# Eight conditioning products moved from the sample attention into the prompt attention of a hybrid decoder step

## The reference

```
def adaln(c, w_ada, b_ada):                       # c: 1 prompt row, 8 sample rows of 1024
    m = jax.nn.silu(c) @ w_ada + b_ada            # w_ada: 1024 x 6144
    return jnp.split(m[:, None, :], 6, axis=-1)   # shift, scale and gate of two norms
...
h = modulated rms_norm(x)                         # uses two of the six parts
y = merge_groups(short_conv(h), nsa_attention(h)) @ w_out
x = x + gate * y                                  # the other four parts from here on
x = x + gate * hier_moe(modulated rms_norm(x))
```

## Time and profile before

| What | us |
|---|---|
| median of 3 runs (2212.95 to 2220.4) | 2215.51 |
| the profiled execution's own time | 2215.07 |
| its span | 2213.3 |
| PE busy (share of the span) | 1931.5 (87%) |
| DVE busy | 1278.9 (58%) |
| ACT busy | 1070.0 (48%) |
| POOL busy | 225.7 (10%) |

### The profile page before, as it was taken

One profiled execution on the slowest core, in us unless ns is written; L12 is line 12 of the kernel. 1 busy time (PEld: TensorE's weight loads), 2 busy tenths in 40 slices (PEclk: granted clock), 3 DMA queues, 4 the chain that ended last, 5 costly groups with the idle time before them and its releaser, 6 DMA issues. The chain is left out here.

```text
span 2213.3 us, 27531 instructions
## 1 busy us (share of the span) xinstructions
PE 1931.5 (87%) x9878; PEld 1497.0 (68%) x9878; DVE 1278.9 (58%) x1961; ACT 1070.0 (48%) x1671; POOL 225.7 (10%) x203
## 2 busy tenths in 40 slices
PE   6899995999979888887976899589999999997756
PEld 2799785999977677772222355468888888885642
DVE  1534424544445667672102566599888888885626
ACT  5312113444436677771110211278788787874532
POOL 0100001000002334330110000001000000000011
PEclk9999997999976799998988999699999999998877
DMA  8321127534037210015881722289999999987636
GB/s 288 78 96 44 48 79 264 217 150 160 8 80 217 63 25 5 6 45 136 244 201 43 285 100 95 105 329 413 425 421 413 415 414 414 412 343 284 248 129 264
DMA packets 155490, 443.05 MB, mean 200 GB/s; under 512 B 37384, under 2 KB 82380, under 8 KB 123712
## 3 DMA queue, kind: packets, MB, share of 16 engines
q1 hardware_dynamic: 136272, 340.82, 41.6%
q0 software_dynamic: 13792, 81.90, 10.8%
q10 hardware_dynamic: 5328, 19.02, 2.1%
HBM read 387.21 MB, written 58.70 MB: 201 GB/s over the span
## 5 line engine op out<-in xcount | busy, mean ns | idle before, releaser
L2782 DVE TENSOR_TENSOR moe_lo<-wts_raw,moe_hi 128x2048 fp32r<-128x2048 f32 x216 | 484.8, 2288 | 115.8 <-ACT moe_hi L2679 115.7
L2679 ACT ACTIVATE moe_hi<-wts_raw 128x2048 fp32r<-128x2048 f32 x216 | 402.7, 1915 | 93.8 <-DMA wts_raw<-in_w_gate 42.7
L949 DVE TENSOR_TENSOR cmp_xl<-cmp_bank,cmp_xh 128x512 fp32r<-128x512 f32 (+1 forms) x136 | 82.6, 668 | 121.0 <-ACT cmp_xh L903 121.0
L873 PE MATMUL cmp_hp<-cmp_xh,cmp_wh 128*128 128x256 f32 (+2 forms) x512 | 150.6, 294 | 0.0
L1375 POOL TENSOR_SCALAR att_prow<-att_prow,att_scale 128x640 f32<-128x640 f32 (+15 forms) x96 | 113.4, 1194 | 342.5 <-DVE att_scale L1499 342.5
L1472 DVE TENSOR_TENSOR att_pl<-att_pT,att_ph 128x512 fp32r<-128x512 f32 (+5 forms) x148 | 101.2, 688 | 79.7 <-ACT att_ph L1403 79.4
L873 PE MATMUL cmp_hp<-cmp_xh,cmp_wl 128*128 128x256 f32 (+2 forms) x512 | 146.6, 286 | 0.0
L873 PE MATMUL cmp_hp<-cmp_xl,cmp_wh 128*128 128x256 f32 (+2 forms) x512 | 146.4, 286 | 0.0
L2550 PE MATMUL moe_G<-moe_hi,moe_xh 128*128 128x512 f32 x288 | 118.1, 410 | 24.8 <-issue 21.7
L1984 POOL DMA_INDIRECT rou_xg<-s_h,rou_idx x36 | 51.2, 1422 | 826.2 <-PE moe_XT L2569 506.7
L2590 PE MATMUL moe_Y<-moe_hi,moe_hh 128*128 128x512 f32 x288 | 115.2, 400 | 19.0 <-issue 11.1
(11 more groups left out here) (455 smaller groups left out, 4391.1 us busy)
## 6 DMA issues: line engine op xcount, KB each, us to landing
wts_raw<-in_w_gate SPq DMA_DIRECT2D x72, 1024.0 KB, 7.0
wts_raw<-in_w_up SPq DMA_DIRECT2D x72, 1024.0 KB, 7.6
wts_raw<-in_w_down SPq DMA_DIRECT2D x72, 1024.0 KB
s_yb<-moe_y ACTq DMA_DIRECT2D x36, 512.0 KB, 7.7
fro_wraw<-in_w_ada SPq DMA_DIRECT2D x4, 2048.0 KB
s_yb<-att_zero SPq DMA_DIRECT2D x1, 8192.0 KB, 32.8
one_buf<-in_w_ada SPq DMA_DIRECT2D x4, 2048.0 KB
smp_wa<-in_w_ada SPq DMA_DIRECT2D x4, 2048.0 KB
```

The costliest lines, as they stand in the source:

```text
L873: last = pe.matmul(hp[u % 2][:, 0:n], lhs[:, w, :], rhs[:, u % 3, at], start=(r == 0 and t == 0 and m == 0), stop=(r == 1 and t == 7 and m ...
L2679: act.activation(hi[p][half][:, :], raw[p][half][:, :], ACT.Copy).then_inc(hi_ready[p], 1)
L2782: dve.tensor_tensor(lo[p][half][:, :], raw[p][half][:, :], hi[p][half][:, :], ALU.subtract).then_inc(lo_ready[p], 1)
```

## The change

The eight pieces leave the sample attention. In the prompt attention they become ring items, two for each pair 6 to 13 (tiles 3 to 6): `("cond", m, 0)` and `("cond", m, 1)`, each with half of a piece's 512 columns. Now 128x128 blocks of `w_ada` are the weights and the nine rows stream, so a half piece is two column blocks by eight row blocks. ACT copies the 128x18 result, DVE adds the bias. The bias arrives as 32 rows of 128 and is turned once at the start (`("bias",)`). After pair 14 the collected columns are turned back (`("mods",)`) and written to `s_mod` in eight transfers. The pieces are loaded into the buffers of the later gathers (`kvs`): the first two at `i == 1` ahead of `sample.load`, the others when the piece two before is through. The sample's compressed keys and values (`ck`, `cv`) and the constant `tri` are loaded in the prompt attention's last tile, into a buffer whose queries and masks are no longer needed; before, they were loaded at the start of the sample attention, or with `sample.load`.

```diff
+    NM, NC9 = ADA - ADA1, 4 * 9
+    P0 = 6
...
     for half in range(2):
         put(("q", 0, half))
+    put(("bias",))
...
             while backs:
-                order.append(("back", backs.pop(0)))
+                pair = backs.pop(0)
+                if 0 <= pair - P0 < NM:
+                    put(("cond", pair - P0, 1))
+                order.append(("back", pair))
+                if pair == P0 + NM:
+                    put(("mods",))
+            if k == 0 and groups[units[y][0]][1] == SEL and 0 <= units[y][0] // 3 - P0 < NM:
+                put(("cond", units[y][0] // 3 - P0, 0))
             for n in mine[len(mine) * k // QG:len(mine) * (k + 1) // QG]:
                 put_tile(n)
...
+            sp.dma_start(brow[:, :], a["b_ada"][:, ADA1 * 512:ADA * 512].rearrange("o (r c) -> (o r) c", c=P)).then_inc(brow_in, 16)
+            sp.dma_start(cT[:, :, :].rearrange("p k n -> p (k n)"), a["s_cT"]).then_inc(cT_in, 16)
+
+            def load_piece(m):
+                if m >= 2:
+                    sp.wait_ge(ring_full, ring_at[("cond", m - 2, 1)] + 1)
+                n = slice((ADA1 + m) * 512, (ADA1 + m + 1) * 512)
+                sp.dma_start(wa[m % 2], a["w_ada"][0, :, n].rearrange("(k p) n -> p k n", p=P)).then_inc(wa_in[m % 2], 16)
...
+                if P0 < 2 * i < P0 + NM:
+                    load_piece(2 * i - P0)
                 if i == 1:
+                    load_piece(0)
+                    load_piece(1)
                     sample.load(nc, a, sp)
...
-            sample.load_modulation(a, sp, tile.ada)
+                if P0 < 2 * i < P0 + NM:
+                    load_piece(2 * i - P0 + 1)
+            sp.wait_ge(ring_full, ring_at[("cond", NM - 1, 1)] + 1)
+            sample.load_compressed(a, sp, tile.buf)
+            sp.wait_ge(ring_free, ring_at[("mods",)] + 1)
+            mod_cols = a["s_mod"][:, ADA1 * 512:ADA * 512].rearrange("r (j x c) -> r x j c", x=8, c=P)
+            for x in range(8):
+                sp.dma_start(mod_cols[:, x, :, :], mrow[x * 9:(x + 1) * 9, :, :]).then_inc(mod_out, 16)
...
+                elif ring[r][0] == "bias":
+                    pe.wait_ge(brow_in, 16)
+                    last = pe.transpose(dst[:, 0, 0:4 * NM], brow[:, :], ident[0:4 * NM, 0:4 * NM])
+                elif ring[r][0] == "cond":
+                    _, m, half = ring[r]
+                    pe.wait_ge(cT_in, 16)
+                    pe.wait_ge(wa_in[m % 2], 16 * (m // 2 + 1))
+                    for t in range(2):
+                        cols = slice((2 * half + t) * P, (2 * half + t + 1) * P)
+                        for k in range(KT):
+                            last = pe.matmul(dst[:, 0, 9 * t:9 * t + 9], wa[m % 2][:, k, cols], cT[:, k, :],
+                                             start=(k == 0), stop=(k == KT - 1))
...
+                elif ring[r][0] == "cond":
+                    _, m, half = ring[r]
+                    at = m * NC9 + 18 * half
+                    act.wait_ge(ring_full, r + 1)
+                    act.activation(mT[:, at:at + 18], src[:, 0, 0:18], ACT.Copy).then_inc(ring_high, 1)
...
-            for m in range(MOD1):
-                condition(m)
...
-                if u in mod_after:
-                    condition(MOD1 + mod_after.index(u))
```

More of the change, by code:

```diff
@@ L1043, in __init__ @@
         self.slot8 = s.sb("slot8", [P, 16])
[L1044 to L1047, removed]
+        self.ck_in = s.sem("ck_in")
+        self.cv_in = s.sem("cv_in")
         self.const_in = s.sem("const_in")
@@ L1202, in stage_prompt_attention @@
         acc = [s.sb(f"acc{i}", [P, NH, HD]) for i in range(2)]
+        wa = [sample.kvs[:, 2 * i:2 * i + 2, :].rearrange("p i c -> p (i c)").rearrange("p (k n) -> p k n", n=512)
+              for i in range(2)]
+        cT = s.sb("cT", [P, KT, 9])
+        brow = s.sb("brow", [4 * NM, P])
+        bT = s.sb("bT", [P, 4 * NM])
+        mT = s.sb("mT", [P, NM * NC9])
+        mrow = s.sb("mrow", [2 * NC9, NM // 2, P])
         S = s.ps("S", [P, NB_S * 512])
@@ L1210, in stage_prompt_attention @@
         q_in = [s.sem(f"q_in{i}") for i in range(2)]
+        cT_in = s.sem("cT_in")
+        brow_in = s.sem("brow_in")
+        wa_in = [s.sem(f"wa_in{i}") for i in range(2)]
+        mod_out = s.sem("mod_out")
         masks_ready = s.sem("masks_ready")
@@ L1292, in fill @@
                         last = pe.transpose(dst[:, t, :], q[i % 2][:, half * 4 + t, :], ident[:, :])
+                elif ring[r][0] == "bias":
[10 more added lines that the diff above has]
+                                             start=(k == 0), stop=(k == KT - 1))
+                elif ring[r][0] == "mods":
+                    pe.wait_ge(ring_free, ring_at[("cond", NM - 1, 1)] + 1)
+                    for j in range(NM // 2):
+                        last = pe.transpose(dst[0:2 * NC9, j, :], mT[:, 2 * NC9 * j:2 * NC9 * (j + 1)], ident[:, :])
                 else:
@@ L1468, in low_part @@
                                              op0=ALU.mult, op1=ALU.subtract).then_inc(ring_free, 1)
+                elif ring[r][0] == "bias":
+                    dve.tensor_copy(bT[:, 2 * NM:4 * NM], src[:, 0, 2 * NM:4 * NM]).then_inc(ring_free, 1)
+                elif ring[r][0] == "cond":
+                    _, m, half = ring[r]
+                    at = m * NC9 + 18 * half
+                    c = 4 * m + 2 * half
+                    dve.wait_ge(ring_free, ring_at[("bias",)] + 1)
+                    piece = mT[:, at:at + 18].rearrange("p (b r) -> p b r", r=9)
+                    dve.tensor_tensor(piece, piece, bT[:, c:c + 2].rearrange("p (b o) -> p b o", o=1).to_broadcast([P, 2, 9]), ALU.add
+                                      ).then_inc(ring_free, 1)
+                elif ring[r][0] == "mods":
+                    dve.tensor_copy(mrow[:, 2:4, :], src[0:2 * NC9, 2:4, :]).then_inc(ring_free, 1)
                 else:
@@ L1568, in stage_sample_attention @@
         tri = given.tri
-        cT = given.cT
-        ones9 = s.sb("ones9", [1, 9])
-        wa = [tile.ada, s.sb("wa1", [P, KT, 512])]
-        ba = [given.ba, s.sb("ba1", [1, 512])]
-        mrow = [s.sb(f"mrow{i}", [9, 512]) for i in range(2)]
         rank = s.sb("rank", [P, NCK])
```

78 lines of the change are left out of this document (20 added, 58 removed).

## The result

The changed kernel takes 2272.72 us (median of 4 runs, 2270.06 to 2276.09), the kernel before beside it 2214.23 us: a ratio of 1.0266, 95% interval 1.0232 to 1.0300. It is slower by 58 us, where the prediction had 27 and a range up to 2262. The profiled execution has a span of 2268.2 us, 54.9 above that of before. Three marks that both traces have divide it into four pieces: the first combine of the prompt attention, its last combine, and the start of the ranking at the sample attention's end.

A forecast was written before the change was run, and what follows sets the result against it. Prediction: work moves from the load-bound sample attention to TensorE-bound prompt-attention tiles; 2215.07 + 5 (bias) + 1.5 (turn) + 86 (conditioning products) - 66 (sample attention) = 2241.6, forecast 2241 us, slower; range 2198 to 2262.

The forecast's parts named there:

- the three places: Prompt attention's start (+5 us), its tiles 3 to 6 with the conditioning products (+86), and the sample attention (-66).
- the mechanism of the lumps: Tiles 3 to 6: each half piece's 32 narrow instructions lower TensorE's clock, so the second close group runs at half; +86 us.
- the third rival: Sample attention: TensorE at a fallen clock also bounds the selected units; gain 52 us instead of 66, time 2255.6; chance 0.15.
- Bias wait: Prompt attention's start: first scores wait behind the bias transpose for the bias load, until 647; +5 us, bounds 0 and 6.
- The lumps' own time: Tiles 3 to 6: a half piece's 32 instructions take 3.42 us at full clock, about 7.0 at half.
- the fourth rival: Tiles 3 to 6: nine columns cost half of 36 and the clock holds; cost 19 us, time about 2175; chance 0.05.
- What lies behind a pair of lumps: Tiles 3 to 6: 3.3 us of ordinary work at half clock after two close half pieces, costing about 1.2 us more.
- The turn at the end: Late prompt attention: four transposes of the collected columns plus copies; +1.5 us, bounds 0 and 3.
- The loads: Prompt attention: piece loads and early `ck`, `cv`, `tri` loads stay hidden; 12 us of cover left for tile 0's store.
- The keys and the gathers: Sample attention: scores start 4.65 us earlier, sixteen gathers at 4.6 us each bound the units; gain 66 us, lower bound 52.

The follow-up runs named there:

- quarter lumps: Changed kernel with each half piece cut into two groups of 16 instructions, spread over four places of a pair: 2245.74 us, 1.0123 of the kernel before.
- 128 columns: Changed kernel with 128 identity columns streaming through the same weights instead of nine conditioning rows: prompt attention 403.6 us; whole time (2108.13 us) not comparable, as conditioning values differ.
- 256 columns: Changed kernel with the nine rows as weights, 256 `w_ada` columns streaming, bias straight into the row buffer, no turn at the end: 2212.54 us, 0.9990 of before.
- the run with dense work: Changed kernel with four unused products of 512 columns added after each of six selected units of the sample attention: 2257.19 us, 1.0195 of the kernel before.
- the run with both findings: Against the kernel before: six pieces in prompt attention with 256 columns streaming, two among the selected units in four parts, no bias turn: 2181.37 us, 0.9834.

## Why the prediction was wrong

The direction, the three places and the mechanism of the lumps were right. Two steps failed, both on the clock. The larger: the prediction let the selected units run at full clock with the gathers as their bound, a gain of 66 us; they ran at half clock, TensorE was the bound, and 52.75 us were gained. The other: it let the clock stay low for only 3.3 us of ordinary work behind a pair of lumps, without a bound; it stayed low for up to 9.5 us, and the stage cost 96.3 us instead of 87.5. With the first alone the time would have been the third rival's 2255.6, inside the range; the second and 5 us behind the ranking carry it past 2262. (The range's top has no sum of its own: 2255.6 with the bias at 6 and the turn at 3 makes 2258.1.)

- **Bias wait.** +5 forecast, 6.1 measured, a tenth above the upper bound. The reading of the earlier trace rows was 1 us early: the slice from 647 to 648 still moves 164 GB/s, so the bytes run until nearly 648, and the wait ended at 647.95.
- **The lumps' own time.** 3.42 us forecast at full clock, 3.57 measured; 7.0 at half, 6.83 measured. All seven second lumps took 6.83. The row with 36 columns was the right price for nine, and the half-priced lumps of the fourth rival do not exist.
- **What lies behind a pair of lumps.** This is the second step that failed. The prediction put 3.3 us of ordinary work at half clock behind a second lump; the nearest figures are the 3.4 us of the earlier trace rows and the 10 us of the earlier trace rows less a lump of 7.0, each from one fall with other work behind it, and the range had no bound for it. In tiles 4 to 6 the whole falls last from 13.6 to 17.0 us (windows of the shortest and of one of the longest):

```profile
830.40:847.40 17.00, 17.00 (x72) 15.22 (x71) 4.62 (x12) 5.95 (x17) 3.74 (x2) 0.50 0.40 134
867.90:881.50 13.60, 13.60 (x60) 12.42 (x60) 3.73 (x10) 4.28 (x13) 3.75 (x2) 0.50 0.40 138
```

  Of these, 9.47 us lie behind the second lump in the first, and 6.5 us (874.80 to 881.30) in the next. With the prediction's own factor (1.2 lost of 3.3, 0.36 of each us) that is an estimate of 2.3 to 3.4 us instead of 1.2. 3.57 + 6.83 + 2.3 to 3.4 us is 12.7 to 13.8; measured are 12.3 to 13.7 from one combine to the next, not 10.6, so hardly any gap was refilled. What sets the length of a fall stays open. DVE's timeline at two combines, before and then after:

```profile
811.64 0.69 DVE L1506 TENSOR_REDUCE att_acc<-att_op 128x256 f32<-128x512 f32 x1
...
934.47 0.69 DVE L1506 TENSOR_REDUCE att_acc<-att_op 128x256 f32<-128x512 f32 x1
```
```profile
838.86 0.69 DVE L1591 TENSOR_REDUCE att_acc<-att_op 128x256 f32<-128x512 f32 x1 [0.55 <-PE att_op L1417]
...
1027.32 0.69 DVE L1591 TENSOR_REDUCE att_acc<-att_op 128x256 f32<-128x512 f32 x1 [0.55 <-PE att_op L1417]
```

  Between them stand five pairs: 188.46 us instead of 122.83, a cost of 65.6 where 53 were forecast. That the whole stage is off by 9 us and not by more is luck: up to tile 3's last combine five lumps cost 21.1 us, where some 27 were forecast, since the kernel before loses time at half clock there itself, and the lone first lump, put at 7.0, took 3.57.
- **The turn at the end.** 1.5 us forecast, within its bounds 0.8 measured: the distance between the last two combines grows by 0.8 us here, and as well with quarter lumps and with 128 columns, where the turn stands too; with 256 columns, where it is gone, it does not grow. The rest of the 2.2 us in the last tile belongs to the lumps' falls.
- **The loads.** Hidden, as forecast: TensorE shows no wait on a piece, and the combine that needs the first tile's stored buffer comes at 754.57, 6.07 us after that of the earlier trace rows, which is the bias wait and nothing else.
- **The keys and the gathers.** The scores came 7.1 us after the last combine instead of 11.8, 4.7 us gained of 4.65 forecast. The gathers' price of 4.6 us was right (4.5 in the run with dense work; and in the run with both findings, where TensorE waits for the last gathers, the loop takes 84.01 us against 81.3). But the prediction took full clock for the units, from a row in which conditioning pieces stood between them, and these were the very instructions that the change takes away. Alone they take 5.13 us, TensorE is the bound, and 52.75 us were gained, not 66. This is the first step that failed. The prediction had it as its third rival, with 52, and gave it 0.15; the argument against it, that there is hardly an idle place, overlooked the 3.18 us at 1067.10 in the trace of before, a wait that is not for a gather. The clock fell around it in both kernels; before, a piece stood behind it and the clock was back at 1076.5, and now nothing brought it back for 76 busy us.
- **Behind the ranking.** +5.2 us in the profiled execution, nothing forecast. The other kernels of this study with the reference's values lie between 1035.0 and 1039.1 there, and before, with 1033.1, lies lowest. What the code there does is unchanged; I take it for scatter, which is argued and not shown.

6.1 + 96.3 - 52.75 + 5.2 = 54.9 us, the whole difference of the spans. Of the some 28 us between forecast and result, 13 are the units' clock, 9 the lumps with what lies behind them, 5 the piece behind the ranking and 1 the bias.

The rule that the prediction set beside the rows, from the Trainium skill (TensorE: Matmul & The Clock Gate, section Part 1: The HAM clock gate), that activity releases the clock and idle time lowers it, does not describe these traces if a busy engine counts as active: 76.00 of 76 us busy at 0.50 among the units, and in the changed kernel falls behind lumps without a gap. The measurement decides.

## What to carry to other kernels

Before work is moved away from a place, ask what it held up there: here the streaming pieces brought TensorE's clock back for their neighbours, and taking them out cost some 13 us of the gain. Nine columns cost here as much as 128 through the same weights (3.57 and 3.66 us a lump), and more than that in the end, as the clock fell behind them; turned round, with the few rows as weights, the same arithmetic cost 41 us instead of 96. A price read from a row holds for the row's neighbours as well: look at what stands between two instructions before their distance is used for another order.

## What the runs showed of the hardware that was not expected

- Useless work made a loop shorter: some 23 us of products with 512 columns streaming, added to the selected units, took 12.6 us off the loop (96.15 to 83.59).
- TensorE ran at 0.50 for 76 us without an idle moment; in the same loop it ran some 15 us at 1.00 with the same units alone, behind four dense products.
- Sixteen narrow instructions in a place (1.75 us) still brought falls: 81.5 us of cost for 32 such lumps, against 96.3 for sixteen of double length.
- 128 columns through the same 32 weight loads took 3.66 us, nine columns 3.57.
- Behind lumps of four narrow instructions the clock still fell twice in tiles 4 to 6, to 0.50 for some 6 us each.
